# ScalarE makes the high parts of sixteen plus sixteen weight tiles, GpSimd only their low parts

## The chip, the cores and the metric

The kernel runs on one core of one Trainium2 chip. The metric is the device time of one execution in microseconds (us); lower is better. Engines are named as in the profile: PE (TensorE matmuls), DVE (VectorE), ACT (ScalarE), POOL (GpSimd), SP (the engine that issues most loads).

## The reference

Two transformer blocks in float32 on 1024 tokens of width 1024. Block 1 is a hybrid layer whose feed-forward ends in `down1`. Block 2, the one that the change touches, is, cut to what matters:

```python
h = rmsnorm(x, g_mix_pre) * (1.0 + scale_m[:, None]) + shift_m[:, None]
z = h @ w_in                                   # includes gl, 3 x 1024 columns
gates = jax.nn.sigmoid(gl).reshape(b, s, N_BRANCH, d)
merged = gates[:, :, 0] * (br_a @ wa) + gates[:, :, 1] * (br_b @ wb) + gates[:, :, 2] * (br_c @ wc)
y = merged @ w_out
x = x + gate_m[:, None] * rmsnorm(y, g_mix_post)
h2 = rmsnorm(x, g_ff_pre) * (1.0 + scale_f[:, None]) + shift_f[:, None]
y2 = jnp.square(jax.nn.relu(h2 @ w_ff1)) @ w_ff2
return x + gate_f[:, None] * rmsnorm(y2, g_ff_post)
```

## The kernel before

**Precision.** The large products are made from operands split in two: a high part, which is the number rounded to the matmul's short float32 form, and a low part, which is the number less its high part. A product is three matmuls: high by high, low by high, high by low.

**Stages.** Each engine runs its own list of instructions, written out by hand in program order, and waits on semaphores. In block 2 two stages go through weights as plain tiles: `upg` (the first gates, from `w_in_2`) and `up2` (the feed-forward's first product, from `w_ff1_2`). Each has 8 steps j of 2 tiles, 16 tiles of 128x1024 weights, called tile 0 to tile 15 here; j = 0 to 3 serve the first half of the tokens, j = 4 to 7 the second half. A tile is 8 times 3 matmuls of 512 columns (`feature_tile`, L1305). After the 16 tiles come groups of seven half-size products ("sevens", class `Sevens`, L485), for which POOL makes four sums and seven low parts a group, and ACT the high parts.

**A weight tile's way.** SP loads it into one of 4 slots of `ring` (L2992). POOL's `split_weight` (L2856) waits for the load and until PE has used the tile three before it, whose place in `w_parts` (3 places) it takes; then it writes the high part with a TENSOR_SCALAR by 1.0 (L2861), which raises the semaphore `weights_high`, and the low part with a subtraction (L2864), which raises `weights_used`. That one wakes PE and frees the slot for the load of the tile four further on.

**What stands around the tiles.** The normalised tokens are turned by PE (`turn_tiles`, L1295, line L1302), shifted by DVE (L2394 in `upg`, L2420 in `up2`), rounded by ACT (L1658, L1665), and their low parts are made by DVE (L2403, L2429). Turns 0 to 3 come before tile 0. Tile 6 is the first tile of step 3; behind it PE waits until ACT has scaled the second half of the tokens (`xhat_half(1)`, L1691; `xhat2_half(1)`, L2000), turns 4, 5 and 6 follow, then tile 7, turn 7 and tile 8. Turn 6 writes the PSUM pair that ACT's step 2 empties. Tile 8 needs, after its first quarter, the low parts of turns 5, 6 and 7 one by one. In that stretch DVE works off, turn by turn: the shift (PSUM to SBUF), two subtractions (L2412 and L2413; L2439 and L2440), and the low part.

**ACT's list.** In `upg`: `high_h` for turns 0 to 3, a square root (L1636), then `gate(j)` (L1859: sigmoid of the two tiles of step j, L1864) and `store_gate(j)` for j = 0 and 1, then four stores of x2 with four square sums (L1673), a square root, `xhat_half(1)`, `gate(2)`, `high_h` 4 to 6, `gate(3)`, `high_h(7)`, and so on. `xhat_half(1)` also waits until the stores of x2 have landed. In `up2`: `xhat2_half(0)`, four square sums straight from PSUM (L2026), each of which lets DVE copy its PSUM pair out (L2765) before turns 0 to 3 can write there; `high_h2` for turns 0 to 3; `relu2(j)` and `store2(j)` (a square, L2044, and a store) for j = 0 and 1; `x3_sums(1)` (four square sums), four stores, `xhat2_half(1)`, `relu2(2)`, `high_h2` 4 to 6, `store2(2)`, `relu2(3)`, `high_h2(7)`.

Of the kernel before, what the change touches and what calls it, by code (L numbers as in the profile page):

```python
# [9 lines left out]
ALU = mybir.AluOpType  # L10
# [36 lines left out]
PLAIN1, PLAIN2 = 2, 4  # L47
# [3 lines left out]

PLAING, GATES7, Z7, Q7 = 4, 8, 4, 2
SEVENSG = GATES7 + Z7 + Q7

STORED1 = 16 + 16 * (PLAIN1 + SEVENS1 // 2)
STORED2 = STORED1 + 16 * (PLAING + SEVENSG)

# [13 lines left out]
def ffn_order(plain, seven, turns, n_plain, n_seven):  # L71
    order = [(plain, j) for j in range(n_plain)]
    order += [(turns, i) for i in range(4, NB)]
    order += [(plain, n_plain + j) for j in range(n_plain)]
    return order + [(seven, g) for g in range(n_seven)]
# [51 lines left out]
ORDER += [("sum1", p) for p in range(7)] + [("turn_h", i) for i in range(4)] + [("down1", 0)]  # L127
ORDER += ffn_order("upg", "seveng", "turn_h", PLAING, SEVENSG)
ORDER += [("fl2", 0), ("fl2", 1), ("qk2", 0), ("qk2", 1), ("v2", 0), ("v2", 1)]
# [110 lines left out]
def program(nc, t, out):  # L240
    L = Ledger()
    with ExitStack() as ctx:
        def sem(name):
            return ctx.enter_context(nc.semaphore(name))
# [26 lines left out]
        def small(name, *shape):  # L271
            return ctx.enter_context(nc.sbuf_tensor(name, list(shape), F32))
# [37 lines left out]
        w_high, w_low = w_parts[:, :, 0, :], w_parts[:, :, 1, :]  # L310
# [60 lines left out]
        ring = small("ring", P, 4, 1024)  # L371
# [35 lines left out]
        def pair(p):  # L407
            return PS[:, 2 * p:2 * p + 2, :]
# [19 lines left out]
        weights_high = sem("weights_high")  # L428
# [56 lines left out]
        class Sevens:  # L485
# [16 lines left out]
            def raw(self, n):  # L502
                g, m = divmod(n, 7)
                a00, a01, _, a11 = self.quarters(g)
                s1, s2, s3, s4 = self.sums
                return (a00, s2, s1, s3, a01, s4, a11)[m]
# [631 lines left out]
        def pool_fill(pe, u):  # L1138
# [6 lines left out]
            else:  # L1145
# [32 lines left out]
        SIG0 = [down1.moved[max(n for n in range(down1.n) if n % 4 == s)] for s in range(4)]  # L1178
        sevensg = Sevens("seveng", SEVENS1, 2 * SEVENS1, 7 * SEVENS1 + down1.n, 4 * SEVENS1 + 4 * K1, SEVENSG, hT_high, hT_low,
                         tx1_high, tx1_low, temps1, sums1)  # L1180
        g2 = SEVENS1 + SEVENSG
        sevens2 = Sevens("seven2", g2, 2 * SEVENS1 + 4 * SEVENSG, 7 * g2 + down1.n, 4 * g2 + 4 * K1, SEVENS2, h2T_high, h2T_low,
                         th2_high, th2_low, temps2, sums2)
# [4 lines left out]
        def part_here(eng, before):  # L1188

            if before is not None:  # L1190
                kind, n, value = before
                if kind == "part":
                    eng.wait_ge(parts_used[n], value)
                else:
                    by_sevens[n].after_step(eng, value)

        def weights_here(pe, stage, i, c):
            pe.wait_ge(weights_loaded[L.slot(stage, i, c)], L.loaded(stage, i, c))
# [10 lines left out]
        def freed(eng, stage, i, u):  # L1209

            eng.wait_ge(psum_free[L.pair(stage, i, u)], L.pair_uses(stage, i, u) + 1)
# [7 lines left out]
        def unit_here(eng, stage, i, u):  # L1219

            kind, n, value = L.full(stage, i, u)
            eng.wait_ge({"weights_used": weights_used, "parts_used": parts_used, "psum_full": psum_full}[kind][n], value)

        def strip(of, b):

            return of[:, 2 * (b % 4):2 * (b % 4) + 2, 512 * (b // 4):512 * (b // 4) + 512]

        def half_of(h):
            return slice(512 * h, 512 * h + 512)
# [379 lines left out]
        def _(act):  # L1609
# [24 lines left out]
            def ln_sqrt_half(r, h):  # L1634
                act.wait_ge(ln_var[r], h + 1)
                act.activation(rstd[:, 4 * h:4 * h + 4], rstd[:, 4 * h:4 * h + 4], ACT.Sqrt).then_inc(ln_sqrt[r], 1)  # L1636
# [17 lines left out]
            def high_h(i):  # L1654
                h, u = divmod(i, 4)
                act.wait_ge(h_shifted[0], i + 1)
                freed(act, "turn_h", i, 0)
                act.copy(hT_high[:, u:KT:4, half_of(h)], x1_first[:, :, u, :] if h == 0 else h_mid[:, u:KT:4, half_of(1)]  # L1658
                         ).then_inc(h_high_made[0], 1)

            def high_h2(i):
                h, u = divmod(i, 4)
                act.wait_ge(h_shifted[1], i + 1)
                freed(act, "turn_h2", i, 0)
                act.copy(h2T_high[:, u:KT:4, half_of(h)], h2_first[:, :, u, :] if h == 0 else h2_mid[:, u:KT:4, half_of(1)]  # L1665
                         ).then_inc(h_high_made[1], 1)

            def high_t(n, high, raw):
                act.copy(high[n - 1][:, :, :], raw[n - 1][:, :, :]).then_inc(t_high, 1)

# [8 lines left out]
            def rms_sqrt_half(r, h):  # L1679
                act.wait_ge(rms_var[r], h + 1)  # L1680
                act.activation(rstd[:, 4 * h:4 * h + 4], rstd[:, 4 * h:4 * h + 4], ACT.Sqrt).then_inc(rms_sqrt[r], 1)
# [124 lines left out]
            for n in (3, 4):  # L1806
                act.wait_ge(t_summed, n - 2)
                high_t(n, tx1_high, tx1_raw)
# [50 lines left out]
            def gate(j):  # L1859
                p = L.pair("upg", j, 0)  # L1860
                unit_here(act, "upg", j, 0)
                if j >= 2:
                    act.wait_ge(hid_stored[j % 2], STORED1 + 16 * (j // 2))
                act.activation(hid1_out[:, j % 2], pair(p), ACT.Sigmoid).then_inc(psum_free[p], 1)  # L1864

            def store_gate(j):
                h, tile = divmod(j, PLAING)
                freed(act, "upg", j, 0)
                act.dma_start(gate_dram[2 * tile:2 * tile + 2, :, half_of(h)].rearrange("t p n -> p t n"), hid1_out[:, j % 2]
                              ).then_inc(hid_stored[j % 2], 16)  # L1870

            for i in range(4):
                high_h(i)
            ln_sqrt_half(1, 1)
            for j in range(2):
                gate(j)
# [46 lines left out]

            for g in range(SEVENSG):
                sevensg.keep_first(act, g)
# [66 lines left out]
            def store_x3(h):  # L1992
                for b in range(4 * h, 4 * h + 4):
                    act.dma_start(x3_dram[tok(b), :].rearrange("p (a n) -> p a n", a=2), strip(y2_at, b)
                                  ).then_inc(x2_stored, 16)

            def xhat2_half(h):
                act.wait_ge(rms_rstd[2], h + 1)
                for b in range(4 * h, 4 * h + 4):
                    act.activation(strip(x2_at, b), strip(y2_at, b), ACT.Copy, scale=rstd[:, b:b + 1]  # L2000
                                   ).then_inc(xhat_made[1], 1)
# [16 lines left out]
            rms_sqrt_half(2, 0)  # L2018
            store_x3(0)
            xhat2_half(0)  # L2020
            for u in range(4):
                p = L.pair("out2", 1, u)
                unit_here(act, "out2", 1, u)
                if u:
                    act.wait_ge(y_moved, u)
                act.activation(junk3.rearrange("p (a n) -> p a n", a=2), pair(p), ACT.Square,  # L2026
                               accum_out=ssq[:, 4 + u:5 + u]).then_inc(y_moved, 1)
            act.wait_ge(y_moved, 4)
            sums_done(1)
            for i in range(4):  # L2030
                high_h2(i)
            rms_sqrt_half(1, 1)

            def relu2(j):
                p = L.pair("up2", j, 0)
                unit_here(act, "up2", j, 0)
                if j >= 2:
                    act.wait_ge(hid_stored[j % 2], STORED2 + 16 * (j // 2))
                act.activation(hid2_out[:, j % 2], pair(p), ACT.Relu).then_inc(psum_free[p], 1)

            def store2(j):
                h, tile = divmod(j, PLAIN2)
# [812 lines left out]
        def _(pool):  # L2855
            def split_weight(stage, i, c):  # L2856
                s, q = L.slot(stage, i, c), L.part(stage, i, c)
                pool.wait_ge(weights_loaded[s], L.loaded(stage, i, c))
                for before in L.part_before[stage, i, c]:
                    part_here(pool, before)  # L2860
                pool.tensor_scalar(w_high[:, q, :], ring[:, s, :], 1.0, 1.0, ALU.mult, ALU.mult  # L2861
                                   ).then_inc(weights_high, 1)
                pool.wait_ge(weights_high, L.splits_before(stage, i, c) + 1)
                pool.tensor_tensor(w_low[:, q, :], ring[:, s, :], w_high[:, q, :].bitcast(F32),  # L2864
                                   ALU.subtract).then_inc(weights_used[s], 1)
# [318 lines left out]
```

## Time and profile before

| | |
|---|---|
| median of 3 runs | 2873.33 us (2866.82, 2873.36, 2873.33) |
| the profiled execution's own time | 2874.97 us |
| its span, first to last instruction | 2873.0 us |
| PE busy | 2768.5 us (96%) |
| DVE busy | 1668.9 us (58%) |
| ACT busy | 1014.2 us (35%) |
| POOL busy | 1123.4 us (39%) |
| mean granted TensorE clock | 0.989 |

The times of the trace are counted from the span's start. The plain tiles of `upg` lie at 1392 to 1493 us, those of `up2` at 2218 to 2323 us. PE is busy in nearly all of the span, so a change can move the end only where PE waits, where its clock is low, or where it would come to wait. Matmuls overlap in the records: one is shown with 0.39 us and the next starts 0.23 us after it.

### The profile page before, as it was taken

The numbers are of one execution on the slowest core, as the hardware profiler recorded it, in microseconds if no ns is written. First come the engines' busy times: TensorE is split into PE (matmuls) and PEld (weight loads), VectorE is DVE, ScalarE is ACT, GpSimd is POOL, SyncE is SP. The second block draws the span as 40 slices with busy tenths as digits, with TensorE's granted clock in tenths as the row PEclk, the third lists the DMA queues.
The fourth block names the chain that finished last, engine by engine and source line by source line (L and its number), as shares of the span: only waits on it lengthen the run. The fifth ranks groups of instructions, "written<-read, shape, count | busy, mean of one in ns | idle before, by whom it ended". The sixth has DMA issues, their size and how long they took to land.

```text
span 2873.0 us, 34107 instructions
## 1 busy us (share of the span) xinstructions
PE 2768.5 (96%) x12618; PEld 2036.0 (71%) x12625; DVE 1668.9 (58%) x2672; ACT 1014.2 (35%) x1750; POOL 1123.4 (39%) x772
## 2 busy tenths in 40 slices
PE   8999999889999999998999999988999899999998
PEld 5444447558888888786778888755557788888886
DVE  0599977665733333699752224666547712235998
ACT  2401026540323333344433332166003444444443
POOL 2000000026687776000677776600216677753020
PEclk9999999999999999999999999999999999999999
DMA  4111136323422221775533335400645433357864
GB/s 115 30 37 37 37 87 187 112 101 99 154 89 82 88 89 64 271 226 191 166 106 118 104 110 176 145 2 7 215 141 180 138 114 106 106 174 225 277 194 169
DMA packets 346212, 363.78 MB, mean 127 GB/s; under 512 B 19768, under 2 KB 250424, under 8 KB 345536
## 3 DMA queue, kind: packets, MB, share of 16 engines
q1 hardware_dynamic: 319920, 283.98, 32.7%
q10 hardware_dynamic: 23648, 70.49, 6.3%
q0 software_dynamic: 2480, 7.13, 1.0%
q8 instruction: 102, 1.67, 0.2%
q14 instruction: 62, 0.51, 0.1%
HBM read 297.45 MB, written 64.09 MB: 126 GB/s over the span
## 4 chain that ended last, share of the span: by engine, by line
PE 80%; DVE 11%; issue 3%; ACT 3%; DMA 2%; ACTq 0%; SPq 0%; DVEq 0%
PE PS L548 29%; PE PS L792 10%; PE PS L1315 9%; PE PS L1279 5%; PE PS L1327 5%; PE PS L1265 4%; PE PS L1556 3%; PE PS L921 3%; PE PS L1396 2%; PE PS L940 2%; PE PS L960 2%; PE PS L1505 2%; PE PS L1369 1%; DVE hid_low L747 1%; DMA arena<-hid_spill 1%
## 5 line engine op out<-in xcount | busy, mean ns | idle before, releaser
L607 DVE TENSOR_TENSOR arena<-arena,PS 128x512 f32<-128x512 f32 x308 | 211.8, 688 | 623.9 <-PE PS L548 622.4
L2861 POOL TENSOR_SCALAR w_parts<-ring 128x1024 fp32r<-128x1024 f32 x98 | 141.0, 1438 | 900.2 <-DMA ring<-in_w_out 275.5
L792 PE MATMUL PS<-w_parts,hid_high 128*128 128x512 f32 x1512 | 471.0, 393 | 17.7 <-DVE w_parts L757 16.3
L792 PEld LDWEIGHTS PS<-w_parts,hid_high 128*128 128x128 f32 x1512 | 283.5, 189 | 84.0 <-DVE w_parts L757 23.9
L548 PE MATMUL PS<-tx_high,w_parts 128*128 128x512 f32 x1024 | 325.8, 389 | 0.0
L792 PE MATMUL PS<-w_parts,hid_low 128*128 128x512 f32 x756 | 295.5, 391 | 0.0
L2864 POOL TENSOR_TENSOR w_parts<-ring,w_parts 128x1024 fp32r<-128x1024 f32 x98 | 277.3, 2829 | 8.2
L586 POOL TENSOR_TENSOR w_parts<-arena,w_parts 128x512 fp32r<-128x512 f32 x176 | 225.0, 1290 | 51.9 <-ACT w_parts L567 51.9
L586 POOL TENSOR_TENSOR w_parts<-ring,w_parts 128x512 fp32r<-128x512 f32 x132 | 170.5, 1292 | 153.0 <-ACT w_parts L567 153.0
L548 PEld LDWEIGHTS PS<-tx_high,w_parts 128*128 128x128 f32 x1024 | 192.2, 188 | 40.0
L719 ACT CAST hid_high<-arena 128x512 fp32r<-128x512 f32 x189 | 117.3, 621 | 251.4 <-PE PS L792 107.8
L548 PE MATMUL PS<-tx_low,w_parts 128*128 128x512 f32 x512 | 199.3, 389 | 0.0
L747 DVE TENSOR_TENSOR hid_low<-arena,hid_high 128x512 fp32r<-128x512 f32 x189 | 137.8, 729 | 75.4 <-ACT hid_high L719 75.3
L2220 DVE TENSOR_SCALAR_CACHE_REDUCE arena<-arena,misc 128x384 bf16<-128x384 f32 (+2 forms) x192 | 171.5, 943 | 2.3
L1030 DVE CUSTOM_DVE_ANT_0 arena<-PS,arena 128x1024 f32<-128x1024 f32 (+7 forms) x160 | 114.8, 755 | 99.7 <-PE PS L928 42.4
L567 ACT CAST w_parts<-arena 128x512 fp32r<-128x512 f32 x176 | 108.5, 618 | 163.6 <-PE PS L548 138.9
L792 PEld LDWEIGHTS PS<-w_parts,hid_low 128*128 128x128 f32 x756 | 142.7, 189 | 30.0
L548 PE MATMUL PS<-x1T_high,w_parts 128*128 128x512 f32 x432 | 138.9, 389 | 0.0
L1279 PE MATMUL PS<-ring,arena 128*128 128x512 f32 (+1 forms) x384 | 138.8, 524 | 0.0
L921 PE MATMUL PS<-arena 64*128 64x512 f32 (+2 forms) x480 | 117.6, 529 | 19.4 <-DVE misc L1030 16.5
L1315 PE MATMUL PS<-hT_high,w_parts 128*128 128x512 f32 x416 | 130.8, 393 | 4.8 <-DVE hT_low L2403 3.6
L2924 POOL CAST arena<-ident 128x128 bf16<-128x128 f32 x1 | 0.3, 289 | 336.8 <-DVE arena L2262 336.8
(355 smaller groups left out, 5636.7 us busy)
## 6 DMA issues: line engine op xcount, KB each, us to landing
arena<-hid_spill SPq DMA_DIRECT2D x216, 256.0 KB, 3.6
ring<-in_w_in SPq DMA_DIRECT2D x84, 512.0 KB, 3.8
hid_spill<-arena ACTq DMA_DIRECT2D x54, 512.0 KB, 2.8
ring<-in_w_gu SPq DMA_DIRECT2D x52, 512.0 KB, 3.9
ring<-in_w_ada SPq DMA_DIRECT2D x48, 512.0 KB, 5.3
ring<-in_w_ff SPq DMA_DIRECT2D x96, 256.0 KB, 3.1
ring<-in_w_ff SPq DMA_DIRECT2D x40, 512.0 KB, 4.1
ring<-in_w_down SPq DMA_DIRECT2D x66, 256.0 KB, 3.0
```

The costliest lines, as they stand in the source:

```text
L548: mm = pe.matmul(self.product(g, m), w[:, at], x[:, k, :], start=(k == 0 and i == 0), stop=(k == 3 and i == 2))
L586: pool.tensor_tensor(low, self.raw(n), high.bitcast(F32), ALU.subtract).then_inc(self.split_low, 1)
L607: dve.tensor_tensor(out, a, self.product(g, m), ALU.add).then_inc(self.combined, 1)
L747: dve.tensor_tensor(self.low[:, n % 4, :], self.tokens(n), self.high[:, n % 4, :].bitcast(F32), ALU.subtract).then_inc(hid_low, 1)
L792: mm = pe.matmul(PS[:, 4 * (p % 2) + u, :], x, w, start=(j == 0 and i == 0), stop=(j == self.n_k - 1 and i == 2))
L921: mm = pe.matmul(PS[:, 2 * m + c // 512, 0:w], self.q(j, m, b), self.k(j, m, c, w), start=True, stop=more[m] is None)
L1279: mm = pe.matmul(PS[:, 2 * p + b % 2, 0:width], source[:, k, tok(b)], ring[:, s, (k % 2) * width:(k % 2 + 1) * width], start=(k == 0), sto ...
L1315: mm = pe.matmul(PS[:, 2 * p + bank, :], w[:, q, k * P:(k + 1) * P], x[:, k, half_of(h)], start=(k == order[0] and n == 0), stop=(k == ord ...
L1327: mm = pe.matmul(PS[:, 2 * p + half, :], x[:, k, at], w[:, q, half_of(half)], start=(first and n == 0), stop=(last and n == 2))
L2220: stepped(dve.tensor_scalar(tested[b], score[b], threshold(column[b]), None, op, ALU.add, accum_out=enough[:, column[b]:column[b] + 1]))
L2861: pool.tensor_scalar(w_high[:, q, :], ring[:, s, :], 1.0, 1.0, ALU.mult, ALU.mult).then_inc(weights_high, 1)
L2864: pool.tensor_tensor(w_low[:, q, :], ring[:, s, :], w_high[:, q, :].bitcast(F32), ALU.subtract).then_inc(weights_used[s], 1)
```

## The change

The high parts of the 32 tiles of `upg` and `up2` leave POOL's `split_weight`; ACT writes them with a copy in a new helper `high_weights(stage, tiles)`. POOL still waits for `weights_high` ahead of each low part. ACT makes tile 0 of `upg` ahead of `high_h(0)`, tiles 1 and 2 behind `high_h(3)`, and tiles 2j+3 and 2j+4 at the end of `gate(j)`, ahead of `store_gate(j)`. In `up2` it makes tiles 0 and 1 behind `xhat2_half(0)`, ahead of the four square sums from PSUM, tile 2 behind `high_h2(3)`, and tiles 2j+3 and 2j+4 at the end of `relu2(j)`, ahead of `store2(j)`.

```diff
+STAGE_STEPS = {"upg": range(2 * PLAING), "up2": range(2 * PLAIN2)}
...
+            def high_weights(stage, tiles):
+                for n in tiles:
+                    i, c = divmod(n, 2)
+                    if i >= len(STAGE_STEPS[stage]):
+                        continue
+                    s, q = L.slot(stage, i, c), L.part(stage, i, c)
+                    weights_here(act, stage, i, c)
+                    if n == 0:
+                        act.wait_ge(weights_high, L.splits_before(stage, 0, 0))
+                    for before in L.part_before[stage, i, c]:
+                        part_here(act, before)
+                    act.copy(w_high[:, q, :], ring[:, s, :]).then_inc(weights_high, 1)
...
                 act.activation(hid1_out[:, j % 2], pair(p), ACT.Sigmoid).then_inc(psum_free[p], 1)
+                high_weights("upg", (2 * j + 3, 2 * j + 4))
...
+            high_weights("upg", (0,))
             for i in range(4):
                 high_h(i)
+            high_weights("upg", (1, 2))
             ln_sqrt_half(1, 1)
...
             xhat2_half(0)
+            high_weights("up2", (0, 1))
             for u in range(4):
...
             for i in range(4):
                 high_h2(i)
+            high_weights("up2", (2,))
             rms_sqrt_half(1, 1)
...
                 act.activation(hid2_out[:, j % 2], pair(p), ACT.Relu).then_inc(psum_free[p], 1)
+                high_weights("up2", (2 * j + 3, 2 * j + 4))
...
                 pool.wait_ge(weights_loaded[s], L.loaded(stage, i, c))
-                for before in L.part_before[stage, i, c]:
-                    part_here(pool, before)
-                pool.tensor_scalar(w_high[:, q, :], ring[:, s, :], 1.0, 1.0, ALU.mult, ALU.mult
-                                   ).then_inc(weights_high, 1)
+                if stage not in ("upg", "up2"):
+                    for before in L.part_before[stage, i, c]:
+                        part_here(pool, before)
+                    pool.tensor_scalar(w_high[:, q, :], ring[:, s, :], 1.0, 1.0, ALU.mult, ALU.mult
+                                       ).then_inc(weights_high, 1)
                 pool.wait_ge(weights_high, L.splits_before(stage, i, c) + 1)
```

## Rows read from the trace of the kernel before

**Rows 1.** Waits of PE, 1375 to 1500 us: who waited for whom, total, times, longest.
```profile
PE PS L1315 <- DVE hT_low L2403: 3.6, 2, 3.2
PE PS L1302 <- ACT arena L1691: 2.3, 1, 2.3
```
**Rows 2.** The same waits of PE, 2155 to 2330 us.
```profile
PE PS L1315 <- DVE h2T_low L2429: 9.8, 5, 3.0
```
**Rows 3.** POOL's two split lines over the span: ns min/median/max.
```profile
L2861 POOL TENSOR_SCALAR w_parts<-ring x98: 1038/1065/3102, 621.0 to 2306.5; 128x1024 fp32r<-128x1024 f32 x98
L2864 POOL TENSOR_TENSOR w_parts<-ring,w_parts x98: 2349/2402/4318, 622.1 to 2307.7; 128x1024 fp32r<-128x1024 f32 x98
```
**Rows 4.** Timeline of POOL: start, us, engine, line, operation, idle before.
```profile
1380.50 2.71 POOL L2864 TENSOR_TENSOR w_parts<-ring,w_parts 128x1024 fp32r<-128x1024 f32 x1
...
1409.50 2.02 POOL L2861 TENSOR_SCALAR w_parts<-ring 128x1024 fp32r<-128x1024 f32 x1
1411.60 3.25 POOL L2864 TENSOR_TENSOR w_parts<-ring,w_parts 128x1024 fp32r<-128x1024 f32 x1
```
**Rows 5.** Timeline of DVE beside it.
```profile
1407.20 3.41 DVE L2514 SCALAR_TENSOR_TENSOR arena<-arena,misc 128x1024 f32<-128x1024 f32 x1
1410.64 1.94 DVE L2516 SCALAR_TENSOR_TENSOR arena<-arena,misc 128x1024 f32<-128x1024 f32 x1
```
**Rows 6.** ACT's rounding copy of the same shape, ns min/median/max.
```profile
L1658 ACT CAST hT_high<-x_first x4: 1047/1051/1053, 1382.5 to 1391.9; 128x1024 fp32r<-128x1024 f32 x4
```
**Rows 7.** POOL in `up2`: two splits as PE frees their places.
```profile
2236.80 1.68 POOL L2861 TENSOR_SCALAR w_parts<-ring 128x1024 fp32r<-128x1024 f32 x1 [0.31 <-PE PS L1315]
...
2242.24 1.55 POOL L2861 TENSOR_SCALAR w_parts<-ring 128x1024 fp32r<-128x1024 f32 x1 [0.44 <-PE PS L1315]
```
**Rows 8.** DVE ahead of the last part of `down1`, timeline.
```profile
1378.23 0.69 DVE L757 TENSOR_TENSOR w_parts<-arena,w_parts 128x512 fp32r<-128x512 f32 x1
...
1379.43 1.52 DVE L757 TENSOR_TENSOR w_parts<-arena,w_parts 128x512 fp32r<-128x512 f32 x1
1380.88 1.52 DVE L2394 TENSOR_SCALAR x_first<-PS,misc 128x512 f32<-128x512 f32 x2
...
1384.41 1.53 DVE L2394 TENSOR_SCALAR x_first<-PS,misc 128x512 f32<-128x512 f32 x2 [2.02 <-PE PS L1302]
```
**Rows 9.** The chain that ended last, `upg`: start, us, what.
```profile
1423.27 5.07 DMA x_spill<-arena
...
1432.75 1.98 PE PS L1302 x8
```
**Rows 10.** Timeline of ACT in `up2`.
```profile
2203.32 4.28 ACT L2000 ACTIVATE arena<-arena,misc 128x1024 f32<-128x1024 f32 x4 [3.30 <-issue]
2207.50 1.00 ACT L2026 ACTIVATE arena<-PS 128x1024 bf16<-128x1024 f32 x1
...
2242.09 1.03 ACT L2039 ACTIVATE arena<-PS 128x1024 f32<-128x1024 f32 x1 [8.75 <-PE PS L1315]
...
2255.68 4.27 ACT L2000 ACTIVATE arena<-arena,misc 128x1024 f32<-128x1024 f32 x4 [4.20 <-issue]
```
**Rows 11.** Timeline of DVE, `up2`: first work after turn 4, last low part.
```profile
2261.14 2.97 DVE L2420 TENSOR_SCALAR h_mid<-PS,misc 128x512 f32<-128x512 f32 x4 [9.45 <-PE PS L1302]
...
2270.35 3.19 DVE L2429 TENSOR_TENSOR h2T_low<-h_mid,h2T_high 128x1024 fp32r<-128x1024 f32 x1
...
2279.06 1.23 DVE L2429 TENSOR_TENSOR h2T_low<-h_mid,h2T_high 128x1024 fp32r<-128x1024 f32 x1
```
**Rows 12.** POOL's one split within that stretch of DVE.
```profile
2268.52 1.19 POOL L2861 TENSOR_SCALAR w_parts<-ring 128x1024 fp32r<-128x1024 f32 x1 [6.47 <-PE PS L1315]
```
**Rows 13.** Timeline of PE behind its waits, `upg` and `up2`.
```profile
1450.13 0.80 PE L1315 MATMUL PS<-hT_high,w_parts 128*128 128x512 f32 x1 [3.17 <-DVE hT_low L2403]
...
2260.00 2.84 PE L1302 MATMUL PS<-ident,arena 128*128 128x128 f32 x24 [1.63 <-ACT arena L2000]
...
2280.34 0.79 PE L1315 MATMUL PS<-h2T_high,w_parts 128*128 128x512 f32 x1 [0.87 <-DVE h2T_low L2429]
...
2285.98 0.39 PE L1315 MATMUL PS<-h2T_low,w_parts 128*128 128x512 f32 x1
```

## The prediction

> **What bounds the kernel now.** First the page: PE is busy 96% of the span, so only PE's waits and its clock can move the end. Then PE's waits in the two stretches that the change touches. In `upg` PE waits 2.3 us for `xhat_half(1)` and 3.6 us for DVE's low parts in tile 8 [rows 1]. In `up2` it waits 9.8 us for DVE's low parts [rows 2] and 1.6 us for `xhat2_half(1)` [rows 13]. It never waits for a weight tile of POOL's in either. So POOL's 1.4 us a tile is not what PE waits for; it counts only through DVE.
>
> How POOL and DVE meet is seen where both work on two SBUF operands [rows 4, 5]. L2514 ends at 1410.61, POOL's TENSOR_SCALAR, begun at 1409.50, ends 0.91 us later; L2516, begun at 1410.64, ends 1.06 us after that (1412.58); POOL's subtraction, begun at 1411.60, ends 2.27 us after that (1414.85). They take turns. I use these net prices: 0.95 us for a high part on POOL, 2.27 us for a low part, 1.1 us for a DVE operation. Alone the two POOL lines show 1.04 and 2.35 us at least, contended 3.10 and 4.32 at most [rows 3]. DVE's shift out of PSUM takes 1.52 us beside POOL's L2864 and 1.53 with POOL idle: it does not take turns [rows 4, 8].
>
> **The change part by part.**
>
> *Removed:* 32 high parts on POOL. *Added:* 32 copies on ACT, 1.05 us each [rows 6], in pairs of 2.1 us. POOL's low part of a tile now waits for ACT, and ACT reaches tile 2j+3 only after its step j. What is queued behind the copies on ACT is named at each place. PE needs 5.44 us a tile (POOL, let go by PE each time, starts at 2236.80 and 2242.24) [rows 7].
>
> *End of `down1`.* The last L757 takes 1.52 us beside POOL's first high part, 0.69 us alone [rows 8]. That high part is ACT's now; PE, which goes on when L757 is done, starts 0.85 us earlier. Gain 0.85.
>
> *The lead of the tiles.* Before, a split starts when the tile three back is used, 10.9 us ahead of need. Now tile 2j+3 has 5.44 us: gate 1.03, copy 1.05, low part 2.35 and some 0.3 of wake-ups are 4.7 us alone, up to 5.8 if DVE holds the port 1.1 us. Bounds per odd tile: 0 and 0.4 us. DVE is busy only at tile 3 of each stage; I take 0.2 in all.
>
> *`upg`, to turn 4.* DVE's eight L2514/L2516 operations share the port with four or five splits; with two low parts instead they end near 1415, not 1423.26 [rows 9]. That gain does not reach PE whole: ACT's step 1 ends where PE's tile 3 ends, its two copies (2.1 us) stand ahead of the four stores and square sums, and `xhat_half(1)` waits for the stores to land. The last store landed 5.07 us after DVE [rows 9]. Now the four are issued one behind another from 1417 to 1420.6, with loads beside them, and I let the last land at 1426 to 1427, against 1428.34. Turn 4 starts 2.2 (bound: 1.3) us earlier, at 1430.5.
>
> *`upg`, turn 4 to tile 8.* Here ACT's copies 7 and 8 stand between `gate(2)` and `high_h(4)`. Low 7 is ready near 1436.3, which is when PE could start tile 7 (1436.89 before). The price is DVE's: its stretch from turn 4 to the last low part, 17.9 us, met one split before (1.4 us lost), and now meets low parts 7 and 8 and, after `gate(3)`, 9 and 10. Low 7 lies mostly under the shifts (0.7 us hit); 8, 9 and 10 hit with 2.27 each less what I can place under a shift. Walking DVE's list I get the end of the stretch at 1455.1 against 1452.7: 2.4 us later although it began earlier. Bounds: all four hidden, 3.6 us earlier; store late and all four hit, 3.4 us later. Value: +2.4.
>
> *`up2`, to turn 4.* Copies 0 and 1 come between `xhat2_half(0)` and the four square sums L2026, and there ACT has no gap: L2000 ends when L2026 starts, at 2207.5 [rows 10]. Both tiles' places are free by then. Square sums, DVE's copies, turns, shifts and low parts follow each other without slack until PE's first matmul at 2217.6, so +2.1. Then copies 5 and 6 come between `relu2(1)` at 2242.09 and the square sums that lead to `xhat2_half(1)` at 2255.68 [rows 10]; PE waits 1.6 us for the latter already [rows 13], so another +2.1. Tile 3 adds 0.1. Turn 4 starts 4.3 us late, after a PE wait of 3.7 us instead of 1.6. In `upg` the 8 transposes of a turn after the 2.3 us wait take 1.98 us [rows 9]; here all 24 take 2.84 [rows 13], so the longer wait can cost 0.9 more. Bounds for the copies: 0 (a gap I don't see) and 4.2.
>
> *`up2`, turn 4 to tile 8.* DVE's stretch lasts 19.2 us, from 2261.14 to 2280.3, and one L2429 of 3.19 us against 1.23 shows the only split in it [rows 11, 12]; 2.7 us of it are that split's. Now low parts 8, 9 and 10 fall into it, 6.8 us: +4.1 net. Bounds: all hidden, -2.7; all four hit, +6.4. Sum at the last low part: 4.3 + 0.9 + 4.1 = 9.3, rounded 9.
>
> *Clock.* After these waits PE runs at 1.2 instead of 2.4 GHz: at 2280.34 one matmul shows 0.79 us, and full pace is back at 2285.98 [rows 13], which costs about 2.8 us; in `upg` from 1450.13 about 1.5. With longer waits ahead, part of the slow stretch falls into matmuls that wait for DVE anyway. I take -1.5 in `up2` and 0 in `upg`; bounds for both together -4.3 and +5.
>
> *Start of the sevens.* Low 15 now waits for `gate(6)`: 1.2 + 1.05 + 2.35, then four sums and a low part of 1.3 each, 11.2 us from the end of tile 13, against 10.9 us of PE work. The 1.3 is a half-size L2864 (half of 2.4 and 0.1) [rows 3]. +0.3 a stage, bounds 0 and 1.
>
> *ACT or POOL elsewhere:* no price; ACT has gaps of 5 to 9 us at every later step.
>
> **The sum,** at the end: `upg` +2.4, `up2` +9 - 1.5, tiles +0.2, sevens +0.6 = +10.7, called +11. The 0.85 gain is inside `upg`'s figure. The profiled execution would go from 2874.97 to 2886; it lies 1.6 above the median of the runs, so the median goes from 2873.3 to 2884.
>
> **A rule beside the rows.** The rows above show turns of a port. The Trainium skill (page "SBUF — State Buffer", section "Who interferes with whom") says the same and adds that ScalarE has ports of its own and waits for nobody. By that rule alone the move is pure gain, since it takes work off the shared port; it is the first rival. No row of before shows where the low parts fall afterwards.
>
> **The rivals.**
>
> *The freed port wins (faster).* Every high part that left POOL frees 0.95 us for DVE, which is PE's bound in both stretches. For it: rows 4, 5 and 8; DVE ends its eight operations 8 us earlier. It needs ACT's copies to be covered in `up2` and the low parts to fall under shifts. Then `upg` ends 3.6 us earlier and saves 1.5 us of clock, `up2` saves 2.7 and some 2.5 us of clock: -10, 2863. It decides once ACT's two pairs cost under 1 us together. Against it: no gap on ACT [rows 10].
>
> *ACT's delay alone.* The low parts fall under the shifts, the copies cost in full: `upg` -3.6, `up2` +5.2 - 2.7, small things +0.8: about 0, 2873. For it: shifts are 6 us of each DVE stretch. Against it: they can cover two low parts, not four.
>
> *The clock stays low too.* The waits in tile 8 become two of over 3 us each, and PE is slow in tiles 8 and 9 as well; all low parts hit: +11 + 7 = +18, 2891.
>
> *The change does not relieve POOL.* Each low part waits for ACT, so POOL is as late as before and DVE meets it equally: the copies on ACT remain, 4.2 + 0.9 us, 2878.
>
> **How the numbers follow.** Forecast 0.48, ACT's delay alone 0.24, slow clock 0.16, freed port 0.07, no relief 0.05. A measurement of this kernel can tell about 0.3% (8.6 us) from no change. Slower by more: 0.16 and 0.42 of the forecast's 0.48, 0.58. Faster by more: 0.06 of the freed port's 0.07. The rest, 0.36, lies within. The range from 2872 to 2892 takes in the forecast, ACT's delay alone, no relief and the slow clock but for their tails, and leaves out the freed port.
>
> **What would show it.** Right: PE waits longer for L2000 (near 3.7 us) and for L2429 (near 14 us); L2026 starts 2.1 us later after L2000; POOL has three or four low parts between turn 4 and tile 8's end, and DVE's L2412, L2440, L2403 or L2429 beside them show 2 to 3.5 us. L757's last is 0.7 us. Wrong: PE waits for L2000 as before, DVE's stretch is under 18 us, or PE waits for POOL's L2864.

## The result, and the profile after

| | before | after |
|---|---|---|
| median | 2873.33 us (2866.82 to 2882.07, 15 runs) | 2882.22 us (2876.93 to 2889.55, 15 runs) |
| span of the profiled execution | 2873.0 us | 2882.1 us |
| DVE busy | 1668.9 us | 1649.9 us |
| ACT busy | 1014.2 us | 1041.3 us |
| POOL busy | 1123.4 us | 1053.6 us |

The ratio is 1.0031 of the medians; with its interval 1.003 [1.0021, 1.0039], so 6 to 11 us slower. The forecast was 2884.0 (2872 to 2892). DVE and POOL do less work than before, and PE ends later.

PE's waits, the first three rows of `upg` (1375 to 1510 us), the others of `up2` (2155 to 2340 us): who waited for whom, total, times, longest. They answer to [rows 1, 2].

```profile
PE PS L1316 <- DVE hT_low L2423: 5.6, 1, 5.6
PE PS L1316 <- POOL w_parts L2885: 2.3, 1, 2.3
PE PS L1303 <- ACT arena L1705: 1.8, 1, 1.8
...
PE PS L1316 <- DVE h2T_low L2449: 11.1, 4, 6.6
PE PS L1303 <- ACT arena L2017: 1.9, 1, 1.9
PE PS L1316 <- POOL w_parts L2885: 1.5, 1, 1.5
PE PS L1303 <- DVE arena L2785: 1.4, 1, 1.4
```

Two things are new. In tile 8 of each stage PE has one long wait for DVE's low part: 5.6 us in `upg`, where the longest was 3.2, and 6.6 us in `up2`, where three waits of 3.0, 2.4 and 0.9 us stood before. And it waits for POOL's low part (tile 7), where it never did. (L2885 is POOL's low part, L1680 ACT's new copy, L2414 and L2440 the shifts, L2423 and L2449 DVE's low parts, L2432, L2433, L2459 and L2460 its subtractions.)

DVE in `upg`, from its first shift after turn 4 to its last low part, and POOL beside it. They answer to the stretch of 17.9 us of the prediction:

```profile
1433.04 2.97 DVE L2414 TENSOR_SCALAR h_mid<-PS,misc 128x512 f32<-128x512 f32 x4 [9.90 <-PE PS L1303]
1435.92 2.24 DVE L2432 TENSOR_TENSOR tx_raw<-h_mid,x_first 128x512 f32<-128x512 f32 x1
1438.20 2.75 DVE L2433 TENSOR_TENSOR tx_raw<-h_mid,tx_raw 128x512 f32<-128x512 f32 x1
...
1443.64 0.68 DVE L2432 TENSOR_TENSOR tx_raw<-h_mid,x_first 128x512 f32<-128x512 f32 x1
...
1447.73 2.35 DVE L2432 TENSOR_TENSOR tx_raw<-h_mid,x_first 128x512 f32<-128x512 f32 x1
1450.11 2.71 DVE L2433 TENSOR_TENSOR tx_raw<-h_mid,tx_raw 128x512 f32<-128x512 f32 x1
...
1455.59 1.23 DVE L2423 TENSOR_TENSOR hT_low<-h_mid,hT_high 128x1024 fp32r<-128x1024 f32 x1
```
```profile
1435.27 5.13 POOL L2885 TENSOR_TENSOR w_parts<-ring,w_parts 128x1024 fp32r<-128x1024 f32 x2 [14.57 <-ACT w_parts L1680]
1447.15 5.13 POOL L2885 TENSOR_TENSOR w_parts<-ring,w_parts 128x1024 fp32r<-128x1024 f32 x2 [6.75 <-ACT w_parts L1680]
```

A subtraction takes 0.68 us alone and 2.24 to 2.75 us beside a low part of POOL's. The four that are held lose 1.56, 2.06, 1.67 and 2.02 us, 7.3 in all, and the stretch is 1433.04 to 1456.8, 23.8 us. Without the holds it would be 16.5; before, it lost 1.4 and lasted 17.9. Both lengths add up.

In `up2` the same is seen. Both hits of the second pair fall on turn 6, on its second subtraction and on its low part, and this is the low part for which PE then waits 6.56 us:

```profile
2271.79 2.77 DVE L2460 TENSOR_TENSOR th_raw<-h_mid,th_raw 128x512 f32<-128x512 f32 x1
...
2282.06 2.86 DVE L2460 TENSOR_TENSOR th_raw<-h_mid,th_raw 128x512 f32<-128x512 f32 x1
2285.03 3.17 DVE L2449 TENSOR_TENSOR h2T_low<-h_mid,h2T_high 128x1024 fp32r<-128x1024 f32 x1
```
```profile
2268.84 5.17 POOL L2885 TENSOR_TENSOR w_parts<-ring,w_parts 128x1024 fp32r<-128x1024 f32 x2 [13.22 <-ACT w_parts L1680]
2282.03 5.09 POOL L2885 TENSOR_TENSOR w_parts<-ring,w_parts 128x1024 fp32r<-128x1024 f32 x2 [8.02 <-ACT w_parts L1680]
```
```profile
2288.26 0.79 PE L1316 MATMUL PS<-h2T_high,w_parts 128*128 128x512 f32 x1 [6.56 <-DVE h2T_low L2449]
...
2292.65 0.40 PE L1316 MATMUL PS<-h2T_low,w_parts 128*128 128x512 f32 x1
```

ACT at the head of `up2`, with the first new pair between the scaling and the square sums, and at step 1, with the pair of tiles 5 and 6. They answer to [rows 10]:

```profile
2206.68 4.27 ACT L2017 ACTIVATE arena<-arena,misc 128x1024 f32<-128x1024 f32 x4 [2.60 <-issue]
2210.86 1.98 ACT L1680 CAST w_parts<-ring 128x1024 fp32r<-128x1024 f32 x2
2212.75 1.01 ACT L2044 ACTIVATE arena<-PS 128x1024 bf16<-128x1024 f32 x1
...
2248.76 1.03 ACT L2058 ACTIVATE arena<-PS 128x1024 f32<-128x1024 f32 x1 [7.01 <-PE PS L1316]
2249.68 1.99 ACT L1680 CAST w_parts<-ring 128x1024 fp32r<-128x1024 f32 x2
```

**Where the 9.1 us of the two spans arise.** I read the start of ACT's work at four points of both traces, since ACT's PSUM step starts when PE ends a pair of tiles:

| point | before | after | later by |
|---|---|---|---|
| `gate(0)` | 1403.31 | 1402.93 | -0.38 |
| `gate(7)` | 1492.66 | 1497.90 | +5.24 |
| `xhat2_half(0)` | 2203.32 | 2206.68 | +3.36 |
| `relu2(2)` | 2259.85 | 2266.77 | +6.92 |
| `relu2(4)` | 2290.05 | 2298.78 | +8.73 |
| `relu2(7)` | 2322.70 | 2331.42 | +8.72 |

In these two executions `upg` costs 5.2 to 5.6 us and `up2` 5.4, and 0.4 more arises behind `relu2(7)`. The 1.9 us that come back between the stages are in code that the change doesn't touch: the way from `gate(7)` to `xhat2_half(0)` took 707.9 to 710.7 us over all the kernels of this study, and before's profiled execution stands at the upper end.

One trace a kernel is not exact to a microsecond. From `gate(0)` to `gate(7)`, the four kernels whose `upg` is as before (before, e2, e9, e10) took 89.4, 92.2, 89.8 and 90.0 us, the three with all of its copies on ACT as in after (after, e1, e5) 95.0, 94.6 and 93.3. From `xhat2_half(0)` to `relu2(7)`, before and e1 took 119.4 and 117.2 us, after, e2 and e6 124.7, 122.8 and 122.9. By these means `upg` costs 3.9 us and `up2` 5.2.

### The profile page after: what moved, and what is told of

Its sections match the earlier page's. It is cut to its first block, busy times and chain, and to the rows that moved or that the text cites. A ratio compares the mean times of both kernels' runs of the same rounds, so it can differ in the third digit from the quotient of the medians.

```text
span 2882.1 us, 34148 instructions
## 1 busy us (share of the span) xinstructions
PE 2769.3 (96%) x12625; PEld 2033.0 (71%) x12625; DVE 1649.9 (57%) x2672; ACT 1041.3 (36%) x1782; POOL 1053.6 (37%) x740
## 3 DMA queue, kind: packets, MB, share of 16 engines
q8 instruction: 102, 1.67, 0.2%
## 4 chain that ended last, share of the span: by engine, by line
PE 80%; DVE 10%; issue 3%; ACT 3%; DMA 2%; POOL 1%; ACTq 0%; SPq 0%; DVEq 0%; POOLq 0%
PE PS L549 29%; PE PS L793 10%; PE PS L1316 9%; PE PS L1280 5%; PE PS L1328 5%; PE PS L1266 4%; PE PS L1557 4%; PE PS L922 3%; PE PS L1397 2%; PE PS L941 2%; PE PS L961 2%; PE PS L1506 2%; PE PS L1370 1%; DVE hid_low L748 1%; DMA arena<-hid_spill 1%
## 5 line engine op out<-in xcount | busy, mean ns | idle before, releaser
L2885 POOL TENSOR_TENSOR w_parts<-ring,w_parts 128x1024 fp32r<-128x1024 f32 x98 | 263.7, 2697 | 391.8 <-ACT w_parts L1680 386.2
L2882 POOL TENSOR_SCALAR w_parts<-ring 128x1024 fp32r<-128x1024 f32 x66 | 86.5, 1310 | 603.2 <-DMA ring<-in_w_out 275.3
L922 PE MATMUL PS<-arena 64*128 64x512 f32 (+2 forms) x480 | 117.7, 530 | 19.2 <-DVE misc L1031 16.4
L991 ACT ACTIVATE arena<-arena,misc 128x1024 f32<-128x1024 f32 (+7 forms) x160 | 123.1, 776 | 21.9 <-DVE misc L1031 21.7
```

What stands on the lines that cost most here:

```text
L922: mm = pe.matmul(PS[:, 2 * m + c // 512, 0:w], self.q(j, m, b), self.k(j, m, c, w), start=True, stop=more[m] is None)
L991: act.activation(p, p, ACT.Exp, bias=rowmin[:, n % 8:n % 8 + 1], scale=-1.0, accum_out=expsum[:, n % 8:n % 8 + 1]).then_inc(self.probs_mad ...
```

## The experiments

The ratios are to the kernel before, run beside them on the same chip (medians 2874.62 us for e1 to e4, 2872.21 for e5 to e8, 2874.08 for e9 to e11). The edit that all share lets each tile have its own maker; ACT also waits for `weights_high` where POOL makes the tile ahead:

```diff
+BY_ACT = {"upg": [...], "up2": [...]}
...
-                    if i >= len(STAGE_STEPS[stage]):
+                    if n not in BY_ACT[stage]:
                         continue
...
-                    if n == 0:
-                        act.wait_ge(weights_high, L.splits_before(stage, 0, 0))
+                    if n == 0 or n - 1 not in BY_ACT[stage]:
+                        act.wait_ge(weights_high, L.splits_before(stage, i, c))
...
-                if stage not in ("upg", "up2"):
+                if 2 * i + c not in BY_ACT.get(stage, ()):
```

Two lengths carry most verdicts: DVE's stretch (its first shift after turn 4 to the end of its last low part of that group) and, in `up2`, two ways of ACT: A from `xhat2_half(0)` to `relu2(0)`, B from `relu2(1)` to `relu2(2)`.

### e1 and e2: one stage at a time

```diff
+BY_ACT = {"upg": [0, 1, 2, 3, 4, 5, 6, 7, 8, 9, 10, 11, 12, 13, 14, 15], "up2": []}   # e1
...
+BY_ACT = {"upg": [], "up2": [0, 1, 2, 3, 4, 5, 6, 7, 8, 9, 10, 11, 12, 13, 14, 15]}   # e2
```

> ScalarE makes the high parts of upg only, up2 is as before. The forecast's split of its sum gives +2.8 us against before for this half; the trace of the changed kernel, read from one event to the next, gives +4.7. If the port theory holds (low parts 7 to 10 hold DVE's second port between turn 4 and tile 8), DVE's stretch there lasts 23 to 24 us against 17.9 and all of the loss lies between turn 4 and the fourth gate. If the copies on ScalarE alone cost, turn 4 starts later than before.

> ScalarE makes the high parts of up2 only, upg is as before. The forecast's split gives +7.9 us; the trace of the changed kernel gives +4.4. The forecast has 4.3 us of it before turn 4 (two pairs of copies on ScalarE's path); the trace of the changed kernel shows about 2.6 there and names a gain that the forecast lacks, DVE's 4-column step ahead of the square root, 1.57 us beside GpSimd before and 0.17 after. DVE's stretch from turn 4: 22 to 24 us against 19.2 by the port theory.

Measured: e1 1.0012 [1.0003, 1.0021], e2 1.0015 [1.0006, 1.0025]: 3.4 and 4.3 us. The stretch of `upg` is 23.5 us in e1, that of `up2` 22.8 us in e2, as in after; the stage left alone keeps 19.2 us (`up2` in e1). The two add up to 7.8 of 8.9 us. Their intervals (0.9 to 6.0 us and 1.7 to 7.2 us) don't tell the two stages apart, nor the forecast's split of e1 from that of the trace; of e2 they leave the trace's 4.4 inside and the forecast's 7.9 outside.

### e3: tiles 7 to 10 back on GpSimd

```diff
+BY_ACT = {"upg": [0, 1, 2, 3, 4, 5, 6, 11, 12, 13, 14, 15], "up2": [0, 1, 2, 3, 4, 5, 6, 11, 12, 13, 14, 15]}
```

> As the changed kernel, but GpSimd makes the high parts of tiles 7 to 10 of both stages again, as early as their places are free. Port theory: low parts 7, 8 and 9 fall ahead of turn 4 again, DVE's stretches go back to about 18 and 19 us, and the time falls to before or some us under it (the gains ahead of turn 4 stay): 2868 to 2874. Theory that the copies on ScalarE's path cost the time: only two of the four pairs in upg and up2 go, the two ahead of up2's turn 4 stay, so 2876 to 2880.

Measured: 1.0001 [0.9992, 1.0011]. The stretches fall to 17.9 and 18.4 us, and PE waits for no low part of POOL's. Eight of the 32 copies bring nearly the whole loss. The two pairs ahead of turn 4 of `up2` stay on ACT here, so they are not it. Whether it is the time of copies 7 to 10 on ACT or where POOL's low parts fall because of them, e4 tells.

### e4: the low parts of tiles 7 to 10 cut to an eighth

```diff
-                pool.tensor_tensor(w_low[:, q, :], ring[:, s, :], w_high[:, q, :].bitcast(F32),
+                w = 128 if stage in ("upg", "up2") and 7 <= 2 * i + c <= 10 else 1024
+                pool.tensor_tensor(w_low[:, q, 0:w], ring[:, s, 0:w], w_high[:, q, 0:w].bitcast(F32),
```

> As the changed kernel, but GpSimd's low parts of tiles 7 to 10 of both stages are 128 columns long instead of 1024 (the other seven eighths are left out, so that stale low parts are used there). ScalarE's copies, their order and every wait stay. Port theory: DVE's stretches fall to 16 to 18 us, time 2866 to 2873. Theory of ScalarE's delay: no change, 2882.

The kernel leaves out seven eighths of these low parts, so it shows times only. Measured: 0.9987 [0.9978, 0.9996], some 12 us under after by the two ratios, with all of ACT's copies in place. POOL in `up2`, three of the four:

```profile
2260.03 0.46 POOL L2887 TENSOR_TENSOR w_parts<-ring,w_parts 128x128 fp32r<-128x128 f32 x1 [12.51 <-ACT w_parts L1681]
2260.98 0.46 POOL L2887 TENSOR_TENSOR w_parts<-ring,w_parts 128x128 fp32r<-128x128 f32 x1 [0.49 <-ACT w_parts L1681]
2270.99 0.46 POOL L2887 TENSOR_TENSOR w_parts<-ring,w_parts 128x128 fp32r<-128x128 f32 x1 [9.55 <-ACT w_parts L1681]
```

The low parts start where ACT's copies put them, as in after, but take 0.46 us instead of 2.4. The stretches are 16.8 and 16.9 us: this is DVE's list with almost nobody beside it. With the low parts in place they are 23.8 and 22.8. So the stretch's growth is POOL's low parts, shown from both sides (moved in e3, cut in e4), and ACT's own time for the copies is not the cause.

### e5 and e10: the two pairs on ACT's path, taken away and alone

```diff
+BY_ACT = {"upg": [0, 1, 2, 3, 4, 5, 6, 7, 8, 9, 10, 11, 12, 13, 14, 15], "up2": [2, 3, 4, 7, 8, 9, 10, 11, 12, 13, 14, 15]}   # e5
...
+BY_ACT = {"upg": [], "up2": [0, 1, 5, 6]}   # e10
```

> As the changed kernel, but in up2 GpSimd makes the high parts of tiles 0, 1, 5 and 6 again: the two pairs of copies that stand on ScalarE's path ahead of up2's turn 4 go. The forecast prices these pairs at 4.2 us, so 2878. The trace of the changed kernel prices the first pair at 1.9 us and the second at 0.6, because DVE's 4-column step (1.57 us beside GpSimd's low part, 0.17 without) takes back most of it: 2880. The stretches behind turn 4 stay as in the changed kernel, 23.8 and 22.8 us.

> ScalarE makes only the high parts of up2's tiles 0, 1, 5 and 6, the two pairs that stand on its path; GpSimd makes all others as before, those of tiles 7 to 10 too. Theory, that each pair delays the chain: xhat2_half(0) to relu2(0) takes 29.8 us instead of 27.9; relu2(1) to relu2(2) takes 18.5 us instead of 17.5 (2.1 for the pair, less 0.6 because VectorE's small step meets less of GpSimd's low part, less some PE slack); the stretch of VectorE stays at 19.2 us. Sum +2.9 us, ratio 1.001. If the copies are hidden: ratio 1.000. If the price is the full 4.2 us: 1.0015.

Measured: e5 1.0016 [1.0007, 1.0025], e10 1.0006 [0.9996, 1.0016]. By the ratios e5 lies about 4 us under after, where the forecast's price gave 4.2 and the trace's 2.5, and e10 lies 1.7 us over before, where 2.9 was expected; with intervals of 2.6 to 2.9 us to either side neither settles the price. The ways are sharper, and in e10 both came as expected. A is 27.85 us in e5 and 27.9 in before, 29.75 in e10 (30.2 in e2 and e6): the first pair costs 1.9 us. B is 15.76 us in e5, 17.76 in before, 18.56 in e10, 18.01 in after. B fell by 2.0 us in e5, though ACT's list in B is the same as before: this was in no step of the forecast. Most of it is a step of DVE on 128x4 elements, between the square sums and `xhat2_half(1)`. Before, with POOL beside it:

```profile
2249.67 1.57 DVE L2444 TENSOR_SCALAR misc<-misc 128x4 f32<-128x4 f32 x1 [6.78 <-ACTq L1677]
```
```profile
2248.82 2.40 POOL L2864 TENSOR_TENSOR w_parts<-ring,w_parts 128x1024 fp32r<-128x1024 f32 x1
```

After, with POOL idle there, since the low part of tile 7 waits for ACT:

```profile
2258.09 0.17 DVE L2464 TENSOR_SCALAR misc<-misc 128x4 f32<-128x4 f32 x1 [14.32 <-ACTq L1691]
```

In e10 the pair moves the square sums 2 us on, and the step meets only the end of the same low part:

```profile
2252.04 1.08 DVE L2465 TENSOR_SCALAR misc<-misc 128x4 f32<-128x4 f32 x1 [11.42 <-ACTq L1692]
```
```profile
2250.70 2.40 POOL L2886 TENSOR_TENSOR w_parts<-ring,w_parts 128x1024 fp32r<-128x1024 f32 x1
```

It ends at 2253.12, POOL at 2253.10; before, 2251.24 and 2251.22. The step waits until POOL's instruction is over, at whatever point it meets it. That is 1.4 of the 2.0 us. Some 0.6 lie behind it, in ACT's issue of the four stores ahead of `xhat2_half(1)`: 4.35 us in before, 3.75 in e5. Nothing here shows why that time varies, from 3.5 to 4.35 us over all the kernels; with the step held as in before, B is 17.3 to 17.5 us in e1, e7 and e8.

### e6 and e7: tiles 7 and 8 earlier, and a mixture

```diff
             sums_done(0)
             rms_sqrt_half(0, 1)
+            high_weights("upg", (7, 8))
...
-                high_weights("upg", (2 * j + 3, 2 * j + 4))
+                if j != 2:
+                    high_weights("upg", (2 * j + 3, 2 * j + 4))
...
+BY_ACT = {"upg": [0, 1, 2, 3, 4, 5, 6, 7, 8, 11, 12, 13, 14, 15], "up2": [3, 4, 11, 12, 13, 14, 15]}   # e7
```

In e6 all 16 tiles of both stages stay on ACT, as in after.

> As the changed kernel, but in upg ScalarE makes the high parts of tiles 7 and 8 ahead of xhat_half(1), where it waits 4.7 us for the stores of x2, and not behind gate(2). Port theory: low parts 7 and 8 are done before turn 4, DVE's stretch in upg falls from 23.8 to 20 to 21 us (low parts 9 and 10 stay in it), PE no longer waits for GpSimd at tile 7, and 3 to 4 us of the 4.7 us that upg lost come back: 2878. Rival: low parts 9 and 10 slide together with other DVE work and nothing comes back, 2882.

> What the runs so far point to: in upg ScalarE makes all tiles but 9 and 10, with 7 and 8 ahead of xhat_half(1); in up2 it makes 3, 4 and 11 to 15, all others stay on GpSimd. Expected from the parts: upg -1.5 to -4 us against before (DVE free ahead of turn 4, stretch 18 us), up2 0 to -1: 2869 to 2873 where before has 2874.6. Rival: the gain ahead of turn 4 is taken by the stores of x2, and it is the same as before.

Measured: e6 1.0022 [1.0013, 1.0031], e7 0.9989 [0.9981, 0.9998]. In e6 low parts 7 and 8 are made from 1420.84, ahead of turn 4, and PE no longer waits for POOL in `upg`; its stretch is 19.9 us with low parts 9 and 10 in it. By the ratios some 2.5 us come back, a little under the 3 to 4 expected and not told from them. With 9 and 10 back on POOL as well (e7) the stretch is 17.9 us, and the time is inside what was expected: a gain of 3 us, just clear of none.

### e8: only the copies behind the stretch

```diff
+BY_ACT = {"upg": [11, 12, 13, 14, 15], "up2": [11, 12, 13, 14, 15]}
```

> Only tiles 11 to 15 of both stages are ScalarE's. GpSimd has 10 high parts less, in a place where DVE's bound work is over. All theories: within 2 us of before; the sevens start up to 0.4 us later a stage. A change of over 3 us would say that something is paid or won behind tile 10 that neither theory has.

Measured: 1.0005 [0.9997, 1.0014], stretches 17.9 and 19.3 us, as before. Ten high parts less on POOL are worth nothing at a place where PE waits for nobody.

### e9 and e11: GpSimd held back for the small step

```diff
             def split_weight(stage, i, c):
                 s, q = L.slot(stage, i, c), L.part(stage, i, c)
+                if stage == "up2" and 2 * i + c == 7:
+                    pool.wait_ge(rms_var[2], 2)
```

e9 is the kernel before with this edit (`BY_ACT` empty), e11 is e7 with it.

> All high parts stay on GpSimd as before; only one thing differs: in up2 GpSimd begins with tile 7 (high and low part) when VectorE's step on four columns that leads to xhat2_half(1) is done. Theory, that this small VectorE step is held by the GpSimd instruction that runs beside it: the step takes 0.17 us instead of 1.57, relu2(1) to relu2(2) on ScalarE takes about 16.2 us instead of 17.3 to 17.8, and the time falls by 1.4 us, ratio 0.9995. Rival, that the step is long for another reason (its wait for the square sums, ScalarE's own end): it stays near 1.5 us and nothing changes. Rival, that GpSimd's later start of tile 7 costs: PE waits for tile 7's or 8's low part, ratio over 1.0005; tile 7's low part would be ready near 2253.5, and PE needs it near 2263.

> The best mixture so far (upg: ScalarE makes all high parts but those of tiles 9 and 10, tiles 7 and 8 before xhat_half(1); up2: ScalarE makes those of tiles 3, 4 and 11 to 15), which gave ratio 0.9989, with GpSimd's tile 7 of up2 held until VectorE's small step is done. If the two gains add: ratio 0.9984, about 2868. If the small step is not on the chain here: 0.9989.

Measured: e9 0.9994 [0.9986, 1.0003]; e11 2867.52 us against 2874.08, 0.9977 [0.9968, 0.9986]. DVE and POOL in e9:

```profile
2250.65 0.17 DVE L2465 TENSOR_SCALAR misc<-misc 128x4 f32<-128x4 f32 x1 [6.73 <-ACTq L1692]
```
```profile
2250.91 1.05 POOL L2885 TENSOR_SCALAR w_parts<-ring 128x1024 fp32r<-128x1024 f32 x1 [3.59 <-DVE misc L2465]
```

The step takes 0.17 us and B 15.84 us (16.2 was expected), as in e5, with no copy on ACT at all. So the gain comes with keeping POOL off the step: 1.4 us are the step itself, the rest is again the issue of the stores, 3.82 us here. In the time of e9 alone the gain is not told from none. e11 beats both kernels: 6.6 us under before by the medians. It is below e7 by 0.0012, where 0.0005 was expected; with the intervals of the two this is not told from 0.0005.

## Why the prediction came out as it did

The sign, the size and the mechanism that was put first held. The sum was +10.7; the two stages show +5.24 and +5.36 in the profiled executions, and the medians differ by 8.9. But the split between the stages was +2.4 and +7.5 (tiles' lead and sevens left out). `upg` was priced too low and `up2` too high, so two errors met, and that the sum came this close is in part luck.

**Right.** Low parts meet DVE after turn 4: POOL has two pairs in each stretch. Each hit costs 1.6 to 2.2 us (but for one of 0.15), a little under the 2.27 priced. The last L757 of `down1` (now L758) takes 0.68 us instead of 1.52; of this PE gains 0.5 (it waits 0.85 us instead of 1.38), not 0.85. L2044 starts 6.07 us after L2017, 4.18 before: 1.9 for the pair, 2.1 priced. ACT elsewhere has no price: from `relu2(4)` to `relu2(7)` nothing is lost (+8.73, +8.72). For the start of the sevens (forecast 0.3 a stage) PE shows no new wait in either stage; a loss that small can't be told from the spread of the traces.

**One of the prediction's own signs of being wrong showed too.** PE waits for POOL's low part of tile 7, 2.3 and 1.5 us. By itself this wait costs nothing: DVE has no gap in either stretch behind it, and it is DVE's last low parts that PE needs in tile 8.

**Wrong, `upg`, +2.4 forecast, +5.2 measured in the profiled pair (3.9 by the means above).** Three terms were off. The first is the start of turn 4, which was to be 2.2 us earlier; `xhat_half(1)` started at 1427.58 instead of 1428.43, so 0.85 earlier:

```profile
1419.00 0.33 ACTq L1699 DMA_DIRECT2D x_spill<-arena  x1
...
1427.58 4.27 ACT L1705 ACTIVATE arena<-arena,misc 128x1024 f32<-128x1024 f32 x4 [4.66 <-DMA x_spill<-arena]
```

The last store was issued at 1419.00, 1.6 us ahead of the 1420.6 assumed, and landed 8.5 us later, past the 1426 to 1427 that I let it have; before, the last one took 5.07 us. The end of DVE's work, 8 us sooner, was not what it waited for; why the store took longer stays open. Against that, the first 8 transposes took 1.11 us instead of 1.98 (granted clock 0.50 before), so DVE's first shift came 1.72 us earlier, and of this error 0.5 us arrives. Second, the stretch grew to 23.8 us where the walk gave 22.6 (1432.5 to 1455.1), 1.2 more: I had low part 7 mostly under the shifts, and it hit a subtraction for 1.56 us. Third, the clock, taken as 0: after the 5.59 us wait the matmuls of tile 8 run at 1.2 GHz (granted clock 0.50) from 1454.21 (0.79 us for the first) to 1459.5, some 5.3 us, 2.6 of them lost, where before lost 1.5. That is 1.1 more, and 2.8 in all.

**Wrong, `up2`, +7.5 forecast, +5.4 measured.** The step that failed is "so another +2.1" for copies 5 and 6. The pair did cost about 1.5 us (B 17.3 in e2 and e6 against 15.8 in e5 and e9), but the same change took POOL's low part of tile 7 off DVE's small step, and gave 1.4 of it back: B is 18.01 us against 17.76 in the two profiled executions, 17.3 in e2 and e6 against 17.3 to 17.5 in e1, e7 and e8. I had priced ports only for DVE's large operations. PE waited 1.87 us, not 3.7, and the 24 transposes took 2.84 us both times, so the 0.9 for a slow turn was nothing. Against that, A grew by 3.3 and not 2.1: the pair alone gives 1.9 (e3, e4 and e10), and the first tile of `up2` ran at 1.2 GHz (granted clock 0.50) from 2225.36 to 2231, 5.6 us, where before it did from 2217.62 to 2221, 3.4 us. The stretch grew by 3.7, close to the 4.1; from `relu2(2)` to `relu2(4)` only 1.8 of it arrive. The clock gave back the rest, as the -1.5 said: before, the slow part begins with the last low part (2280.34 to 2285.98), now it begins 2.6 us ahead of it (2288.26 to 2292.65), in matmuls that would have waited for DVE anyway.

**The rivals.** The freed port was real (the small step, the last L757, DVE's eight operations, which end at 1414.65 instead of 1423.25), and e7 and e11 show a gain once the low parts are kept out of the stretches. In the change itself the hits in the stretches outweigh it. ACT's delay alone is refuted as the whole: e3 keeps both pairs ahead of turn 4 of `up2` and stands at 1.0001, and e4 keeps all copies and stands below before. The slow clock as that rival had it, with two waits of over 3 us in tile 8, is not seen: each tile 8 has one long wait. No relief is refuted by DVE's busy time, 19 us less. The Trainium skill (page "SBUF — State Buffer", section "Who interferes with whom") was right about ACT, whose pairs of copies take 1.98 or 1.99 us in all these rows, with POOL and DVE at work or not; that the move is then pure gain does not follow, because POOL's remaining half now starts when ACT is done.

## What to carry to other kernels

When half of an engine's job moves to another engine, ask when the remaining half will now run, and lay its duration over the critical engine's list there. Here tiles 7 to 10, whose low parts had filled the two stretches, carried nearly all of the 8.9 us (e3). Keep the shared port quiet around the work that PE waits for, even by holding an engine back, and place or leave the copies one by one; a mixture of both kernels with one hold (e11) was faster than either. Small steps on a chain deserve a look of their own, since a 0.17 us step can cost 1.6.

## What the runs showed of the hardware

**A turn is a whole instruction, for small and large DVE operations alike.** The 128x4 TENSOR_SCALAR ended 0.02 us after POOL's subtraction, having met it at two different points (1.57 and 1.08 us), and took 0.17 us with POOL idle or held. The large ones show the same: the subtraction of 1438.20 ended at 1440.95, 0.55 us after POOL's pair of low parts (it takes 0.69 alone), and the low part of 2285.03 ended at 2288.20, 1.08 us after POOL's (1.23 alone). In all three, DVE's own work ends behind POOL's by its length alone less some 0.15 us. So what a hit costs is what is left of POOL's instruction when DVE comes to it, less that 0.15 us, whatever DVE's own size: 1.56 us for the subtraction that came 0.65 us into a low part, 2.06 us for the one behind it, which met a low part at its start.

**The same waits, a different clock.** Before, e9 and e10 run the same code in the stretch of `up2`, and their first wait in tile 8 is 3.0 us each time. What differs is where PE's granted clock falls to 0.50, at which a matmul of 512 columns shows 0.63 to 0.79 us instead of 0.39. Before:

```profile
2277.68 0.50 PE L1315 MATMUL PS<-h2T_high,w_parts 128*128 128x512 f32 x1 [2.44 <-DVE h2T_low L2429]
...
2280.34 0.79 PE L1315 MATMUL PS<-h2T_high,w_parts 128*128 128x512 f32 x1 [0.87 <-DVE h2T_low L2429]
...
2285.98 0.39 PE L1315 MATMUL PS<-h2T_low,w_parts 128*128 128x512 f32 x1
```

In e9:

```profile
2276.83 0.79 PE L1317 MATMUL PS<-h2T_high,w_parts 128*128 128x512 f32 x1 [1.43 <-DVE h2T_low L2450]
...
2280.01 0.40 PE L1317 MATMUL PS<-h2T_low,w_parts 128*128 128x512 f32 x1
```

In e9 the slow part begins before the second wait and eats it (1.43 us instead of 2.44); in before and e10 it begins about the last wait, and matmuls that nobody holds run at half pace, in before until 2285.98. The way from `relu2(2)` to `relu2(4)` is 30.2 and 30.3 us in before and e10, 27.9 in e9, 27.8 in e8. So some 2.4 us of a single profiled execution go with where the slow part falls, which is as much as several terms of the forecast. This is why small verdicts here rest on medians and on durations of DVE and ACT. What decides where it falls is not shown.
